# Moving work between engines and queues at the start and in the decode attention of a one-core decoder layer

## The reference, cut to what matters

```
h = rmsnorm(x, norm_mix);  proj = h @ w_in          # 256 prompt tokens and 8 sequences x 8 new tokens
q, k, v, z, xbc, dt, glu, gates = columns of proj
a = stick_breaking_attention(q, [cache_k[pages], k], [cache_v[pages], v])   # 1024 cached keys a sequence
b = mamba2(z, xbc, dt, state_ssm);  c = conformer(glu, state_cf_conv)
x += (sum over branches of sigmoid(gate) * (branch @ w_branch)) @ w_out
x += hier_moe(rmsnorm(x));  x += sigmoid(rmsnorm(x) @ w_ple_gate) * (p @ w_ple_proj);  y = rmsnorm(x)
# stick breaking: z = q.k/8 + bias; w = exp(log_sigmoid(z) + sum over later keys of log_sigmoid(-z))
```

## Time and profile before

| | us |
|---|---|
| median of 3 runs (930.21 to 930.57) | 930.53 |
| the profiled execution's own time | 929.8 |
| its span (first to last instruction) | 928.1 |
| PE busy | 851.9 |
| DVE, ACT, POOL busy | 408.2, 219.9, 132.6 |

### The profile page before, as it was taken

How to read it: one execution, slowest core, us unless ns; L and a number is a source line. 1 busy time by engine, 2 the same in 40 slices (tenths; PEclk the granted TensorE clock), 3 DMA queues, 4 the chain that set the end, 5 groups by cost and what they waited for, 6 DMA issues and landing times.

```text
span 928.1 us, 12213 instructions
## 1 busy us (share of the span) xinstructions
PE 851.9 (92%) x4496; PEld 512.9 (55%) x4496; DVE 408.2 (44%) x974; ACT 219.9 (24%) x432; POOL 132.6 (14%) x249
## 2 busy tenths in 40 slices
PE   6699999999778959999999999879999999999895
PEld 3377767666556636556456767644444444433473
DVE  3306665366466362434302421533454354444553
ACT  0211443323332132233214002421111111100233
POOL 5002059999200000000000020000000000000000
PEclk9799999999979979999999999999999999999998
DMA  9323222322972344787855400079997998999701
GB/s 268 96 91 111 96 95 90 114 91 75 281 221 60 114 136 132 222 263 255 261 206 183 148 1 1 0 282 370 423 420 314 422 421 360 421 380 418 302 0 60
DMA packets 79695, 190.37 MB, mean 205 GB/s; under 512 B 9001, under 2 KB 33897, under 8 KB 67335
## 3 DMA queue, kind: packets, MB, share of 16 engines
q1 hardware_dynamic: 74448, 184.40, 54.0%
q0 software_dynamic: 1600, 4.34, 1.7%
q10 hardware_dynamic: 3583, 0.80, 0.5%
HBM read 184.23 MB, written 5.64 MB: 205 GB/s over the span
## 4 chain that ended last, share of the span: by engine, by line
PE 67%; POOL 11%; DVE 7%; DMA 3%; ACT 3%; SPq 3%; ACTq 3%; issue 2%; DVEq 0%; POOLq 0%
PE bank L2238 13%; PE bank L1866 9%; POOL ring L613 8%; PE bank L1693 7%; PE bank L2258 6%; PE bank L2035 6%; PE bank L2075 4%; PE bank L2149 4%; PE bank L2202 3%; PE bank L1979 3%; POOL proj L616 2%; PE bank L1931 2%; PE bank L1949 2%; SPq L383 1%; DMA gate_w<-in_w_in 1%
## 5 line engine op out<-in xcount | busy, mean ns | idle before, releaser
L1693 PE MATMUL bank<-scratch,ring 128*128 128x320 f32 x512 | 144.2, 438 | 0.0
L2238 PE MATMUL bank<-weights,h_exp 128*64 128x512 f32 (+1 forms) x864 | 127.0, 492 | 3.6 <-DMA weights<-in_w_expert_up 3.6
L1866 PE MATMUL bank<-scratch,gate_w 128*128 128x320 f32 x384 | 115.5, 457 | 9.1 <-DMA gate_w<-in_w_in 8.3
L1693 PEld LDWEIGHTS bank<-scratch,ring 128*128 128x128 f32 x512 | 96.4, 192 | 43.2 <-issue 5.6
L1866 PEld LDWEIGHTS bank<-scratch,gate_w 128*128 128x128 f32 x384 | 75.5, 202 | 42.8 <-DMA gate_w<-in_w_in 9.6
L1565 DVE TENSOR_TENSOR x<-x,bank 128x320 f32<-128x320 f32 x160 | 67.1, 482 | 52.2 <-PE bank L2202 52.2
L2238 PEld LDWEIGHTS bank<-weights,h_exp 128*64 128x64 f32 (+1 forms) x864 | 39.7, 122 | 67.8 <-issue 60.9
L613 POOL TENSOR_SCALAR ring<-scratch,par_w 128x64 f32<-128x64 f32 x120 | 71.2, 625 | 3.0
L2258 PE MATMUL bank<-weights,act_ft 128*64 128x512 f32 (+1 forms) x432 | 61.0, 486 | 0.4 <-DVE act_ft L1582 0.4
L1152 DVE SCALAR_TENSOR_TENSOR proj<-scratch,par_w,proj 128x256 f32<-128x256 f32 x120 | 53.5, 510 | 0.2
L639 POOL MEMSET scratch<- 16x2048 f32 x1 | 1.8, 1795 | 301.8 <-DVE proj L1420 301.8
(11 more groups left out here) (366 smaller groups left out, 1108.6 us busy)
## 6 DMA issues: line engine op xcount, KB each, us to landing
weights<-in_w_expert_gate SPq DMA_DIRECT2D x32, 1024.0 KB, 10.0
weights<-in_w_expert_up SPq DMA_DIRECT2D x32, 1024.0 KB, 12.0
weights<-in_w_expert_down SPq DMA_DIRECT2D x16, 2048.0 KB, 15.2
ring<-in_w_in SPq DMA_DIRECT2D x8, 2048.0 KB, 7.8
ring<-in_cache_k SPq DMA_DIRECT2D x64, 256.0 KB, 4.0
ring<-in_cache_v SPq DMA_DIRECT2D x64, 256.0 KB, 4.2
gate_w<-in_w_in SPq DMA_DIRECT2D x24, 512.0 KB, 6.5
ring<-in_w_branch SPq DMA_DIRECT2D x3, 2048.0 KB, 8.9
```

Source lines behind the costliest of these rows:

```text
L1693: m = MM(bank[b_][:, 0:T], slot(j, DC, GROUP)[:, k, (n % 4) * P:(n % 4 + 1) * P], h[:, k, :], start=k == 0, stop=k == DC - 1)
L1866: m = MM(bank[b_][:, c0:c0 + T], g_w[GW_AT[g]][:, k, :], h[:, k, :], start=k == 0, stop=k == DC - 1)
L2238: m = MM(bank[0][per * p:per * (p + 1), 0:2 * DE // g], h_exp[i % 2][:, k, first_place(n):first_place(n) + per], w_gu[u][:, :, k, columns( ...
```

## The change

- x comes in two halves of 512 features (four transfers, of which PE waits for the first two, and for the others ahead of chunk 4). ACT squares the chunks, DVE adds them in pairs, PE sums four pairs. PE transposes the parameters (norms and convolution weights) ahead of the sum, ACT loads its table ahead of the squares and copies the parameters ahead of the root.
- dt_bias and a_log are issued by SP ahead of `w_group(0)`, the other small transfers by SP behind `w_group(1)`; query_bias becomes eight transfers of 16 rows. ACT waits for them behind the dt work instead of ahead of it.
- The decode scores run in four column groups of 32 query rows (two heads of two sequences each), accumulated over the two sequences. The rows of scores, weights and the mask are ordered by head pair, sequence, head, token. `weights_copy` undoes that order with two copies instead of one for each PSUM bank.
- Gate tiles 10 and 11 move from the second turn's two places to the end of the first turn, ahead of `turn_keys(1, 0)`; tile 10 goes to PSUM bank 2, and `gate_weights(11)` is issued ahead of `keys(1, 1)`.

```diff
-    GATE_BANK = [(6, 0)] * 7 + [(4, P)] * 17
+    GATE_BANK = [(6, 0)] * 7 + [(4, P)] * 3 + [(2, 0)] + [(4, P)] * 13
...
+        def by_sequence(out, in_, u):
+            return (out.rearrange("p (g u c n) -> p g u c n", u=2, c=WC, n=2 * NT)[:, :, u],
+                    in_.rearrange("p (g c u n) -> p g c u n", u=2, c=WC, n=2 * NT)[:, :, :, u])
...
         def _(sp):
-            sp.dma_start(x_tok[:, 0:2, :], a["x_prompt"][0].rearrange("(b p) d -> p b d", p=P)
-                         ).then_inc(s("x_loaded"), 16)
-            sp.dma_start(x_tok[0:TS, 2, :], a["x_sample"].rearrange("b t d -> (b t) d")
-                         ).then_inc(s("x_loaded"), 16)
+            for name, f in (("x_loaded", slice(0, D // 2)), ("x_rest_loaded", slice(D // 2, D))):
+                sp.dma_start(x_tok[:, 0:2, f], a["x_prompt"][0].rearrange("(b p) d -> p b d", p=P)[:, :, f]
+                             ).then_inc(s(name), 16)
+                sp.dma_start(x_tok[0:TS, 2, f], a["x_sample"].rearrange("b t d -> (b t) d")[:, f]).then_inc(s(name), 16)
...
+            sp.dma_start(dt_bias, a["dt_bias"][0].unsqueeze(1)).then_inc(s("w_dt_loaded"), 16)
+            sp.dma_start(a_log, a["a_log"][0].unsqueeze(1)).then_inc(s("w_dt_loaded"), 16)
             w_group(0)
             w_group(1)
+            for r in range(8):
+                sp.dma_start(query_bias[2 * NT * r:2 * NT * (r + 1), :],
+                             a["sb_bias"][0, r // 2 * 2:r // 2 * 2 + 2].unsqueeze(1).broadcast_to((2, NT)),
+                             allow_slow_non_contiguous=True).then_inc(s("small_loaded"), 16)
...
             keys(1, 0)
+            gate_weights(11)
             keys(1, 1)
-            gate_weights(11)
...
-            act.wait_ge(s("x_ready"), DC)
+            act.preload_act_table_set("natural_log_exp_and_others")
+            for c in range(DC):
+                act.wait_ge(s("x_ready"), c + 1)
+                F(h[:, c, :], x[:, c, :], ACT.Square).then_inc(s("norm_squared"), 1)
+            act.wait_ge(s("par_turned"), 2)
...
-            act.wait_ge(s("small_loaded"), 16 * 11)
+            act.wait_ge(s("w_dt_loaded"), 16 * 3)
...
+            act.wait_ge(s("small_loaded"), 16 * 15)
             for n in range(1, 5):
                 evacuate(n)
...
+            def pair(c):
+                dve.wait_ge(s("norm_squared"), c + 2)
+                TT(h[:, c, :], h[:, c, :], h[:, c + 1, :], ALU.add).then_inc(s("norm_paired"), 1)
...
-                rows_of = [slice(u * DH, (u + 1) * DH) for u in range(2)]
-                for c in range(WC):
-                    for u in range(2):
-                        m = MM(bank[2 + hf][rows_of[u], :], q_cur[:, u, c * 64:(c + 1) * 64], k_feat[:, u, c, :],
-                               start=c == 0, stop=c == WC - 1)
+                rows_of = [slice(4 * NT * c, 4 * NT * (c + 1)) for c in range(WC)]
+                for u in range(2):
+                    for c in range(WC):
+                        m = MM(bank[2 + hf][rows_of[c], :], q_cur[:, u, c, :], k_feat[:, u, c, :], start=u == 0, stop=u == 1)
...
                 score(i, 1)
+                if i == 0:
+                    pe.wait_ge(s("z_biased"), 1)
+                    gate_tile(GATES_OF[1][0])
+                    pe.wait_ge(s("z_biased"), 3)
+                    gate_tile(GATES_OF[1][1])
```

More of the change, by code:

```diff
@@ L576, in _ @@
                      ALU.not_equal, 0.0))
-            ch.add(where(m4, [[NT, NB], [0, H], [1, NT]], -1, -1, ALU.is_ge, 0.0))
+            ch.add(where(mask_own[:, :, :], [[NT, NB], [1, NT]], -1, -1, ALU.is_ge, 0.0))
             ch.add(where(seq_s, [[NT, NB], [1, NT]], 0, -1, ALU.is_ge, 0.0))
             ch(where(own_seq[:, :], [[NT, NB]], NT - 1, -1, ALU.is_ge, 0.0))
+            for u in range(2):
+                for e in range(2):
+                    row = 2 * NT * u + NT * e
+                    ch.add(pool.tensor_copy(
+                        mask_new[:, :, :].rearrange("s i (c n) -> s i c n", c=WC)[:, :, :, row:row + NT],
+                        mask_own[:, u:NB:2, :].unsqueeze(2).broadcast_to((TS, NB // 2, WC, NT))))
+            ch.wait()
             pool.sem_inc(s("masks"), 1)
@@ L917, in weights_copy @@
                     act.wait_ge(s("w_turned"), 3 * i + turned_)
-                    copy(probs_t[:, k0:k0 + n], b_[:, 0:n]).then_inc(s("turned_copied"), 1)
+                    for u in range(2):
+                        done = copy(*by_sequence(probs_t[:, k0:k0 + n], b_[:, 0:n], u))
+                    done.then_inc(s("turned_copied"), 1)
             def o_copy(i):
@@ L1109, in _ @@
                 dve.tensor_copy(x[:, c, :], bank[c % 4][:, 0:T]).then_inc(s("x_ready"), 1)
-                dve.wait_ge(s("x_ready"), c + 1)
-                TT(h[:, c, :], x[:, c, :], x[:, c, :], ALU.mult).then_inc(s("norm_squared"), 1)
+                if c % 2 == 0 and c:
+                    pair(c - 2)
+            pair(DC - 2)
             norm_inverse(0, D)
@@ L1654, in norm_sum @@
                 m.then_inc(s("norm_summed"), 1)
-            pe.wait_ge(s("const"), 2)
-            for c in range(DC):
-                norm_part(0, h, c, DC, 0)
             pe.wait_ge(s("par_loaded"), 13 * 16)
@@ L1667, in _ @@
             m.then_inc(s("par_turned"), 1)
+            pe.wait_ge(s("const"), 2)
+            for c in range(0, DC, 2):
+                pe.wait_ge(s("norm_paired"), c // 2 + 1)
+                m = MM(bank[7][:, 0:T], ones[:, :], h[:, c, :], start=c == 0, stop=c == DC - 2)
+            m.then_inc(s("norm_summed"), 1)
             pe.wait_ge(s("x_ready"), DC)
```

86 lines of the change are left out of this document (48 added, 38 removed).

## The result

The changed kernel takes 918.71 us (median of 5 runs, 910.75 to 919.64) against 930.57 for the kernel before: a ratio of 0.986, with its 95% interval in brackets [0.9831, 0.9888]. It is faster, but by 11.9 us and not by 26.0, and 918.71 lies above the forecast range (898 to 914). The profiled execution is the fastest of the five: 910.75 us, span 909.0. So two things are to be explained: why this execution gained 19.1 us of span and not 26, and why the others gained less still.

What follows compares the result with a forecast made beforehand. PE was taken to hold two thirds of the chain, time being won where it stands still or its work shortens. Start 10.3 plus decode 15.7 makes 26.0 off the profiled 929.8: 903.8, median 904.5 us, range 898 to 914.

Steps and rivals of the forecast that it cites:

- if the 13 parameter transfers have landed ... I take 13.8 or earlier: Start: parameter transfers landed by 13.8, so PE's parameter transposes follow x's without waiting and end at 15.9.
- a sum that I took too short: Start: sum of squares in 8 instructions instead of 16 takes 2.6 us (2.3 to 3.8), ready at 18.5.
- The first rival: Start: parameters land only at 21.86 and hold the sum; root 3.2 earlier, start gives 3.7, time 911; chance 0.11.
- the forecast 10.3: Start: whole gain 10.3 us (3.2 to 13), from the root 9.8 earlier and dt 0.5 shorter.
- Decode up to the second weighing: Decode attention: PE is 16.0 us ahead at the end of turn three's `weigh`.
- the 6.6 forecast: Decode turn one: turn two's first half score starts 6.6 us earlier, right behind DVE's last key copy.
- gate tile 21 starts 41.6 us after that `weigh`: Decode, last turn: SP's fetches set gate tile 21's start, 41.6 us instead of 42.8 after the weighing; gain only 1.2.
- I charged 1.5: Decode, gate tile 21: PE's lower clock after standing still 3 us costs 1.5 us (0 to 1.5).
- the signs of being wrong: Included a new wait for keys or gate weights in turns two and three, where shorter turns leave SP less slack.
- Column groups without gain: Rival, decode scores: four column groups no faster than two; 18.6 us gained in all, time 912; chance 0.06.
- Nothing from moving transfers off ACT: Rival, start: transfers and root as late from SP; only decode's 15.7 gained, time 914.8; chance 0.03.
- Small transfers late on SP: Rival, start: ACT stands ahead of `evacuate(1)`; slower than before if they land after 78, 937 at 85; chance 0.06.

Runs made afterwards that it cites:

- the three profiles: The changed kernel profiled three times, unedited the second and third time: medians 918.71, 913.82 and 916.40 us.
- the three edits: Changed kernel; convolution state counted apart, first 4 MB of weights held until parameters land, gate tiles 21 and 22's weights issued amid the last two value fetches: 900.92 us.
- two column groups: Changed kernel with the decode scores in two column groups again, start and gate tiles as changed: 917.71 us, ratio 0.987.
- The early gate weights: Changed kernel with gate tile 21's weights issued between the last turn's two value fetches (also "gate 21 early"): 908.29 us.
- the start alone: Kernel before with only the change's start (x halves, ACT squares, pair sums, small transfers behind SP's weights), query_bias as before: 924.70 us, ratio 0.9959.
- filling: Throwaway PE matmuls in routing gaps and ahead of first expert: changed kernel 913.26 (5, 11, 16), 908.83 (2, 5, 8); with the three edits and dt filled 897.71, 898.35.

## Why the prediction was wrong

**The start: the step that failed is "if the 13 parameter transfers have landed ... I take 13.8 or earlier".** They let PE go at 19.08, 20.51 and 18.07 in the three profiles. In the first profile the root comes 6.1 us later than forecast (24.66 for 18.6): 5.2 for these transfers, 1.5 for a sum that I took too short, less 0.6 for shorter transposes. The first rival came true, by chance almost to the number: the root 3.7 earlier, where the rival said 3.2 (1.7 and 4.2 in the other two profiles). The sign that I missed was in the diff: all thirteen are counted by one semaphore, the last is 480 KB, and 4 MB of weights go out beside it. Holding the weights back brought the transfers to 14.67 and the start's gain to 7.2. With the three edits it was 10.5, so some 10 us were there to be won; but that this is the forecast 10.3 is luck, two wrong sizes that cancel. The root came 8.8 earlier (19.60) and not 9.8, and dt took 4.47 instead of 6.23, which is 1.8 off and not 0.5. The sum, put at 2.6 us for eight instructions, took 3.97 to 4.63 in every execution of the changed start, and 4.01 in the kernel with the three edits, where PE came to it without a gap and the windows of its trace give a granted clock of 1.00; the runs do not show why. What held: x at 5.8 (6.5 forecast), the transposes' end at 14.1 (13.85), and what tile 0 gained reached the first key page, give or take a few microseconds (5.5 and 5.1 here; 3.2 and 7.1 with two column groups).

**Decode up to the second weighing: right.** Forecast 16.0, measured (420.76 - 298.29) - (399.4 - 293.21) = 16.3 (15.4 and 15.2 in the other two profiles). The steps of it show: scores of 1.9, the first of turn two at 338.28 (11.5 earlier, the start's 5.1 among it, so 6.4 for the 6.6 forecast), the second right behind the copies (0.99 of idle time for 0.85).

**Decode behind it: the step that failed is "gate tile 21 starts 41.6 us after that `weigh`".** It was 44.9. SP came out of the keys' fetch and its gate weights only at 400.8, 1.4 us after the weighing; the value fetch took 13.87 to issue instead of 12.52; the weights took 6.6 to land instead of 5.98. That is 3.3 us, and the tile lost 3.0 to the lower clock where I charged 1.5. 16.3 - (44.9 - 42.8) - 3.05 = 11.1, which is what the table has. I saw that SP takes over, but took its time from turns in which PE was the slower one, and had it free at the weighing; with PE 16 us ahead SP had no slack left in these turns. The prediction names this loss of slack among the signs of being wrong, but its sum has nothing for it. The early gate weights bear it out: 19.9.

**The median is not the profiled run.** I set the median 0.7 above the profiled execution. For the changed kernel the first five runs lay up to 9 us above it. Adding the smallest gain of each stretch in the three profiles (1.6 + 10.0 - 0.1 = 11.5, a span of 916.6) nearly reaches the upper end of the runs; which stretches were slow in those five runs was not profiled. The Trainium skill ("TensorE: Matmul & The Clock Gate", "Part 1: The HAM clock gate") says that the number of matmuls at the lower clock at a kernel's start differs from run to run of one kernel. The traces agree: dt took 4.47 us in one execution of the changed kernel and 6.16 in two, and in the middle the 12 matmuls of the input projection took 3.50, 4.92 and 5.19.

**The other rivals.** Column groups without gain: refuted (1.92 against 3.65). Nothing from moving transfers off ACT: refuted, since the root came at 24.66 and 23.57 (changed kernel, start alone), while ACT issued transfers until 27.09 before, and the start alone is faster, 0.9959 [0.9931, 0.9987]; but half of what was hoped for went to landing times. Small transfers late on SP: they were late (query_bias took 14.04 us to issue, pages went out at 31.46) but ACT copied tile 1 out at 42.13 without a wait for them.

What stays open: what makes the clock fall in a given execution and not in another, why the sum of squares is slow, and why the same kernel gave 918.7, 913.8 and 916.4.

## What to carry to other kernels

When a step is moved ahead, look at every transfer that its wait counts. Here the largest, issued last, set the time; with a count of its own, and 4 MB of bulk loads still beside it, the next one (62 KB) let PE go at 16.68 in one execution and at 14.43 in another. Holding the bulk back until the small ones were in did about as much as counting apart (root at 20.83 against 22.84 and 20.16, medians 910.34 and 911.44); with both, in three kernels, PE came to these transfers without a wait (root at 19.60 in the first). When PE's work is shortened, follow the queue that feeds it to the end of the stage: here 7 to 10 of the 20 us of the decode attention were lost because one 512 KB load stood behind sixteen page fetches, and issuing it ahead of the last eight gave them back there (5.5 us in the median). A forecast for a median needs more than one profile where PE has short gaps.

## What the runs showed of the hardware

- Short gaps have a price that varies by execution. The 12 matmuls of the input projection stand behind gaps of some 0.7 and 1.4 us. In the 14 profiled executions without filling there (every kernel of this document, before included) they took 3.50 us in three and 4.92 to 6.55 in eleven; in the four with filling they took 3.50 each time. This is where most of the rest's gains and losses in the table come from: from the branches to the end of the first 32 expert matmuls it took 133.3 to 135.0 us in those three, 136.3 to 140.8 in the eleven and 136.0 to 138.0 with filling, and what follows took 300.5 to 303.1 in all. Windows of PE in the kernel with gate 21 early (stretch, its length, busy time of PE, PEld, DVE, ACT and POOL, then PE's clock, DMA share and GB/s; a clock of 1.00 is 2.4 GHz, 0.50 is 1.2) show nearly the lower level (0.53) in the first stretch, the full one in the second, with PE busy all the time in both:

```profile
580.00:586.50 6.50, 6.48 (x13) 3.81 (x12) 5.66 (x13) 0.87 (x2) 0.00 (x0) 0.53 0.00 0
588.00:594.00 6.00, 5.90 (x43) 5.76 (x43) 0.00 (x0) 3.21 (x8) 0.00 (x0) 1.00 0.80 284
```

- A transfer of 480 KB took 11.4 to 15.3 us to land beside 4 MB of weights of another queue (twelve traces), and 8.8 to 9.8 with these held back (four); x's two halves of 512 KB, issued ahead of both, took 4.9 to 5.4 either way.
